# Norm boundaries in two token groups: the last out and down units run once per group, no constant matmuls, five buffers for rounded weights instead of three

## The reference

```python
def rms_norm(x, g):
    y = xf * lax.rsqrt(jnp.mean(jnp.square(xf), axis=-1, keepdims=True) + NORM_EPS)
...
        h_l = modulate(rms_norm(x, g_pre_mix), mod_l[0], mod_l[1])
        p_l = split_proj(h_l @ w_in[l])
...
        y_l = merge_branches((gla_l, att_l, lru_l), p_l[11], w_branch[l], w_out[l])
        x = x + mod_l[2] * rms_norm(y_l, g_post_mix)
...
        h_l = modulate(rms_norm(x, g_pre_ffn), mod_l[3], mod_l[4])
        x = x + mod_l[5] * rms_norm(conv_ffn(h_l, ffn_w_up[l], ffn_conv_w[l], ffn_conv_b[l], ffn_w_down[l]), g_post_ffn)
```

## Time and profile before

| | |
|---|---|
| median of 3 runs | 1924.03 us (1923.77 to 1925.73) |
| the profiled execution, its span | 1924.9 us |
| TensorE busy | 1858.9 us, 97% |
| weight loads (overlap TensorE) | 1545.5 us, 80% |
| VectorE busy | 1343.7 us, 70% |
| ScalarE busy | 990.0 us, 51% |
| transfers | 247.17 MB, mean 128 GB/s |
| mean granted TensorE clock | 0.993 |

### The profile page before, as it was taken

One profiled execution on the slowest core, in us unless ns is written; L12 is line 12 of the kernel. 1 busy time (PEld: TensorE's weight loads), 2 busy tenths in 40 slices (PEclk: granted clock), 3 DMA queues, 4 the chain that ended last, 5 costly groups with the idle time before them and its releaser, 6 DMA issues.

```text
span 1924.9 us, 26001 instructions
## 1 busy us (share of the span) xinstructions
PE 1858.9 (97%) x10504; PEld 1545.5 (80%) x10504; DVE 1343.7 (70%) x1934; ACT 990.0 (51%) x1405; POOL 18.9 (1%) x51
## 2 busy tenths in 40 slices
PE   7999999999999999899999998999999999989998
PEld 4778777777778887578888885778778888979997
DVE  5666546635677887878888797756556688678864
ACT  4543345555665323554444236543446887466663
POOL 1000000000000000000000000000000000000000
PEclk9999999999999999999999999999999999999999
DMA  8211212223244555234444563222323554535653
GB/s 340 70 56 56 72 55 66 77 82 97 90 142 132 181 190 186 98 103 150 164 164 152 188 218 108 77 66 66 93 66 99 155 162 150 183 114 186 181 182 120
DMA packets 68374, 247.17 MB, mean 128 GB/s; under 512 B 7696, under 2 KB 8736, under 8 KB 68128
## 3 DMA queue, kind: packets, MB, share of 16 engines
q1 hardware_dynamic: 65600, 235.96, 37.0%
q0 software_dynamic: 2080, 7.47, 1.3%
q10 hardware_dynamic: 576, 2.10, 0.3%
HBM read 244.44 MB, written 1.05 MB: 128 GB/s over the span
## 4 chain that ended last, share of the span: by engine, by line
PE 72%; DVE 18%; ACT 6%; issue 3%; POOL 0%; ACTq 0%; DVEq 0%; POOLq 0%
PE ps L1499 53%; DVE wlo L842 5%; PE ps L1489 4%; PE ps L1529 2%; DVE fa L892 2%; ACT whi L443 2%; PE ps L1774 2%; PE ps L1869 2%; PE ps L1795 1%; DVE state L1225 1%; PE ps L1707 1%; PE ps L1685 1%; DVE xc L892 1%; PE ps L1786 1%; PE ps L1646 1%
## 5 line engine op out<-in xcount | busy, mean ns | idle before, releaser
L842 DVE TENSOR_TENSOR wlo<-wraw,whi 128x1024 fp32r<-128x1024 f32 x352 | 429.5, 1222 | 235.0 <-ACT whi L443 234.6
L443 ACT ACTIVATE whi<-wraw 128x1024 fp32r<-128x1024 f32 x352 | 370.3, 1054 | 221.8 <-PE ps L1499 208.9
L1499 PE MATMUL ps<-hh,whi 128*128 128x512 f32 (+1 forms) x1632 | 369.3, 348 | 7.3 <-DVE fa L892 3.2
L1499 PE MATMUL ps<-hl,whi 128*128 128x512 f32 (+1 forms) x1632 | 366.0, 346 | 0.0
L1499 PE MATMUL ps<-hh,wlo 128*128 128x512 f32 (+1 forms) x1632 | 335.1, 346 | 1.9 <-DVE wlo L842 1.9
L1499 PEld LDWEIGHTS ps<-hh,whi 128*128 128x128 f32 x1632 | 269.6, 190 | 49.1 <-issue 9.1
L1499 PEld LDWEIGHTS ps<-hl,whi 128*128 128x128 f32 x1632 | 271.2, 190 | 37.6 <-issue 1.6
L1499 PEld LDWEIGHTS ps<-hh,wlo 128*128 128x128 f32 x1632 | 262.7, 190 | 41.1 <-issue 4.4
L870 DVE SCALAR_TENSOR_TENSOR ps<-wada,cond 128x1024 f32<-128x1024 f32 x144 | 173.4, 1246 | 0.0
L892 DVE SCALAR_TENSOR_TENSOR fa<-ps,par,fa 128x510 f32<-128x510 f32 (+1 forms) x176 | 100.1, 610 | 17.2 <-ACT fa L522 15.7
L1499 PE MATMUL ps<-bh,whi 128*128 128x512 f32 (+1 forms) x384 | 88.7, 353 | 0.0
(11 more groups left out here) (300 smaller groups left out, 2592.7 us busy)
## 6 DMA issues: line engine op xcount, KB each, us to landing
wraw<-in_weights SPq DMA_DIRECT2D x352, 512.0 KB, 3.6
wada<-in_w_ada_rows SPq DMA_DIRECT2D x80, 512.0 KB, 3.5
ada_first<-in_w_ada SPq DMA_DIRECT2D x14, 512.0 KB, 16.3
wgate<-in_w_gate POOLq DMA_DIRECT2D x16, 256.0 KB, 2.9
x<-in_xt ACTq DMA_DIRECT2D x2, 512.0 KB, 7.7
x<-in_xt SPq DMA_DIRECT2D x2, 512.0 KB, 7.1
ada_first<-in_w_ada ACTq DMA_DIRECT2D x2, 512.0 KB, 12.5
wdec<-in_w_dec POOLq DMA_DIRECT2D x2, 512.0 KB, 4.8
```

Source lines behind the costliest of these rows:

```text
L443: A_(whi[u % HI][:], wraw[RING_W[u] % RAW][:], ACT.Copy).then_inc(s_hi, 1)
L842: V.tensor_tensor(wlo[s][:], wraw[s][:], whi[u % HI][:].bitcast(F32), ALU.subtract).then_inc(s_lo, 1)
L1499: ins = mm(dst[:, r, c:], w[:, kk, r * P:(r + 1) * P], x_[:, UK * h + kk, c:], start=h == 0 and k in (0, 2) and kk == 0, stop=h == m - 1 a ...
```

## The change

The tokens at a boundary are cut in two groups (`group_of`): context and latent tokens in layer 0 (256 columns each), the two halves of the latent tokens in layer 1 (128 columns each). Each group has its own sums, roots and walk. `last_pair` computes group 0 of the last out or down units, its sums, then group 1 of the last 2 (out) or 3 (down) units; the earlier three units of down run both groups one after the other. The two groups use different PSUM bank pairs. `next_pairs` takes both first pairs through all eight tiles for group 0, then for group 1, with group 1's sums between the first tiles. The constant matmuls are gone. `HI` goes from 3 to 5, for which GpSimd's descriptor scratch becomes smaller. The output leaves in eight transfers of half the size. The low-rank product of gqk moves behind both groups.

```diff
-RAW, HI, LEAD = 7, 3, 2
+RAW, HI, LEAD = 7, 5, 2
+SPLIT = {"out": 2, "down": 3}
...
+        def group_of(m, g):
+            size = CTX if m < 2 else SEQ // 2
+            a = TOK - (2 - g) * size
+            return slice(a, a + size), a // CTX
...
# ScalarE
+                last_tiles(0)
...
+                hi(LATE[m])
+                first_root(0)
+                next_root(0)
+                h(0, 0)
+                h(0, 1)
+                h(0, 2)
+                last_tiles(1)
+                hi(u0 + 2)
+                h(0, 3)
+                h(0, 4)
+                first_root(1)
+                hi(u0 + 3)
+                h(0, 5)
+                h(0, 6)
+                next_root(1)
+                h(0, 7)
+                for k in range(KT):
+                    h(1, k)
...
# VectorE
+                last_cross(0)
                 lo(LATE[m])
...
+                next_sum(0)
+                tile(0, 0)
+                for k in range(1, KT):
+                    tile(0, k)
+                    low(0, k - 1)
+                    if k == 4:
+                        last_cross(1)
+                    if k == 3:
+                        lo(u0 + 2)
+                    if k == 5:
+                        lo(u0 + 3)
+                    if k == 6:
+                        next_sum(1)
+                tile(1, 0)
+                low(0, KT - 1)
+                for k in range(1, KT):
+                    tile(1, k)
+                    low(1, k - 1)
+                low(1, KT - 1)
...
# TensorE, last_pair
-                steps = [(v, k) for ks in ((0, 1, 4), (2, 3, 5)) for v in (u - 1, u) for k in ks]
-                for v, k in steps:
-                    part(v, k)
+                early, late = range(PAIR_UNIT[PAIR_AT[l, name, 3]], u - SPLIT[name] + 1), range(u - SPLIT[name] + 1, u + 1)
+                for v in early:
+                    for g in range(2):
+                        for k in range(6):
+                            part(v, k, g)
+                for v in late:
+                    for k in range(6):
+                        part(v, k, 0)
                 pe.wait_ge(s_adat, len(ADA_MIX) if (l, name) == (0, "out") else len(ADA_TILE))
+                pe.wait_ge(s_acc, 2 * m + 2)
                 for bank, j in banks:
-                    early_sum(l, name, bank, j)
-                    last_sum(l, name, bank, j)
-                if len(banks) == 3:
-                    pe.wait_ge(s_par, 16)
-                    for _ in range(5 if c0_of(l) == 0 else 3):
-                        mm(ps[:, 4, :], ones[:], par[:].rearrange("p l n -> p (l n)")[:, 0:512], start=True, stop=True)
+                    gathered_sum(l, name, bank, j)
+                    last_sum(l, name, bank, j, 0)
+                for v in late:
+                    for k in range(6):
+                        part(v, k, 1)
...
# TensorE, next_pairs
+                one(1, 0, (0,), 0)
+                one(1, 1, (0,), 0)
+                one(1, 0, (1, 2), 0)
+                last_sum(l, name, 6, 0, 1)
+                one(1, 1, (1, 2), 0)
+                for k in range(2):
+                    one(0, k, (0, 1, 2), 0)
+                last_sum(l, name, 7, 1, 1)
+                last_sum(l, name, 5, 2, 1)
+                both(2, (0,), 0)
+                for k in range(2, KT):
+                    if k + 1 < KT:
+                        both(k + 1, (0,), 0)
+                    both(k, (1, 2), 0)
+                both(0, (0,), 1)
+                for k in range(KT):
+                    if k + 1 < KT:
+                        both(k + 1, (0,), 1)
+                    both(k, (1, 2), 1)
+                if n % 2 == 0:
+                    low_rank(n // 2)
```

More of the change, by code:

```diff
@@ L577, in boundary @@
                 squares, scaled_squares, _ = sums_of[name][2]
[L578 to L585, removed]
-                    A_(scaled_squares[:, 0, c0:], branches[:, 0], ACT.Square).then_inc(s_tsq, 1)
-                    hi(LATE[m])
@@ L588, in boundary @@
[L588 to L598 removed]
+                branches = (mixed if name == "out" else y2)[:, 6:8]
@@ new lines, in tile, with low @@
+                def tile(g, k):
+                    c, _ = group_of(m, g)
+                    branch_tile(m, k, src, name, c)
+                    residual_tile(m, g, k, src, c)
+                    scaled_tile(n, g, k, dst, c, root2[name])
+                def low(g, k):
+                    low_tile(n, g, k, dst, group_of(m, g)[0])
+                if m == 2 * DEPTH - 1:
+                    for g in range(2):
+                        c, _ = group_of(m, g)
+                        dve.wait_ge(s_r1, 2 * m + g + 1)
+                        for k in range(0, KT, 2):
+                            two = src[:, k:k + 2, c]
+                            V.tensor_tensor(two, two, root1[name][:, None, c].broadcast_to([P, 2, c.stop - c.start]), ALU.mult)\
+                                .then_inc(s_ym, 2)
+                            dve.wait_ge(s_ym, x_count(m, g, k + 1))
+                            V.tensor_tensor(x[:, k:k + 2, c], x[:, k:k + 2, c], two, ALU.add).then_inc(s_x, 2)
+                    return
@@ L1474, in part @@
                 if k == 0:
-                    if h == 0 and q >= 2:
+                    if h == 0 and group == 1:
+                        pe.wait_ge(taken[(q + 1) % 2], (q + 1) // 2)
+                    elif h == 0 and q >= 2:
                         pe.wait_ge(taken[j], q // 2)
@@ new lines, in last_sum @@
+            def last_sum(l, name, bank, j, g):
+                m = 2 * l + (name == "down")
+                c, _ = group_of(m, g)
+                ready_, n, done = ((s_sq, 2 + 2 * m + g + 1, s_stat), (s_sqp, 5 * m + 4 + g, s_cs),
+                                   (s_xy, 5 * m + 4 + g, s_bs))[j]
+                pe.wait_ge(ready_, n)
+                if g and m < 2 * DEPTH - 1:
+                    pe.wait_ge(s_S, 2 * m + 1)
+                elif g:
+                    pe.wait_ge(s_r1, 2 * m + 1)
+                for t in range(2):
+                    ins = mm(ps[:, bank, c], ones[:], sums_of[name][2][j][:, t, c], start=False, stop=t == 1,
+                             skip_group_check=True)
+                ins.then_inc(done, 1)
@@ new lines, in last_pair, with next_pairs, one, both @@
+                for v in late:
+                    for k in range(6):
+                        part(v, k, 1)
+                if m == 2 * DEPTH - 1:
+                    last_sum(l, name, 6, 0, 1)
+            def next_pairs(u, n):
+                l, name = (n - 1) // 2, "down" if n % 2 == 0 else "out"
+                def one(p, k, which, g):
+                    tile_part(u + 2 * (k // UK) + p, k % UK, n, which, g)
+                def both(k, which, g):
+                    for p in range(2):
+                        one(p, k, which, g)
+                one(1, 0, (0,), 0)
+                one(1, 1, (0,), 0)
+                one(1, 0, (1, 2), 0)
+                last_sum(l, name, 6, 0, 1)
+                one(1, 1, (1, 2), 0)
[15 more added lines that the diff above has]
+                    low_rank(n // 2)
```

310 lines of the change are left out of this document (158 added, 152 removed).

## The result

The changed kernel took 1955.76 us (median of four executions, 1952.45 to 1972.59) against 1924.88 (1923.77 to 1926.41): ratio 1.0175, 95% interval 1.015 to 1.02. That is 31 us slower where 12 were forecast, and above both ranges, 1928 to 1943 and the wider 1917 to 1944. The profiled execution, with a span of 1970.6 us, is the slowest of the four, so its losses are read at their largest; a second profile stands with the experiments.

A forecast was written before the change was run, and what follows sets the result against it. TensorE was taken as the bound, busy 1858.9 of 1924.9 us. Terms -1.5 - 3.0 + 5.5 + 12.9 - 2.0 = +11.9 gave a span of 1936.8, so 1936 us; range 1928 to 1943, 8 in 10 within 1917 to 1944.

The forecast's parts named there:

- B0: Boundary in layer 0, out to up: the groups were to gain, -1.5 us.
- B1: Boundary from layer 0 down to layer 1 gqk: the groups were to gain, -3.0 us.
- B2: Boundary in layer 1, out to up, now 128 columns: the groups were to lose, +5.5 us.
- B3: The end, behind down of layer 1, now 128 columns: the groups were to lose, +12.9 us.
- walk of VectorE 31 us: Layer 0: VectorE's walk over sixteen half tiles was to take 31.0 us against 26.0 before.
- At B2 TensorE without gaps: Expected profile in layer 1, out to up: TensorE sets the pace, VectorE waits; stretch ends at 1739.6 against 1734.07.
- The price of a 128-column matmul: Layer 1's last two boundaries: 0.115 us per matmul, between 0.107 (weight load alone) and 0.120 (with fixed part).
- 81 ns for a sustained matmul of 128 columns: Skill page's figure, an estimate by which the sum would be about 1922 us instead of 1936; no row showed it.
- Five buffers: Rounded weights: ScalarE stops waiting for TensorE before rounding the next unit; -2.0 us (0 to -5).
- Constants: Multiplied constants taken out at three boundaries: their time lies in TensorE's wait for the walk, so 0.
- a slower mode of the short matmul itself: Rival: short matmuls cost 0.22 us as in float32, 58 us more, 1994; chance 13%.

The follow-up runs named there:

- five_buffers_alone: The kernel before with five rounded-weight buffers and the smaller queue scratch, constants kept, no groups: 1923.30 us, ratio 0.999.

## Why the prediction failed, step by step

The direction and the price were right; the time was 19 us above the forecast. Two terms, B0 and B1, had the wrong sign and make 11.4 us of that: B0 came 6.7 us above its term and B1 4.7. B2 makes 2.3 us at full clock and, in the median execution, some 5 more through the half clock (1955.76 against 1950.85 with the pause filled). B3 gives 0.7 back. So two steps failed: "walk of VectorE 31 us", and "At B2 TensorE without gaps" together with the full clock that was assumed there.

- **The price of a 128-column matmul**, 0.115: measured 0.112, and the same at 64 and 192 columns, so the reason given (the weight load) holds. The prediction said that the trace does not show 128 columns; its transposes do, with 0.110. The Trainium skill's 107 ns for a load (TensorE: Matmul & The Clock Gate, section LDWEIGHTS (loading the stationary operand)) agrees; its 81 ns for a sustained matmul of 128 columns (section Back-to-back issue gap), by which 1922 would have come out, does not: here the measurement decides.
- **B3**, +12.9: measured +12.2.
- **B0**, -1.5: +5.2. Sums and the walk's start came as forecast. The walk was 3.8 longer, of which 1.98 + 0.32 + 0.82 are waits for ScalarE. Its rounding of a unit now stands behind group 1's tiles; the order on ScalarE was in the diff and I did not price it. The half clock behind the 3.94 us pause cost 2.9, where 1.4 stood in the sum. With rounding moved and the pause filled, B0 took 55.8 us instead of 58.5, the walk 32.1 instead of 34.8, and the 2.9 were gone.
- **B1**, -3.0: +1.7. The walk's start came as forecast here too, and the walk was 4.4 longer, with the same waits of VectorE for ScalarE in it (2.31 + 0.32 + 0.82). The longer walk is nearly the whole difference of 4.7. Only B0's waits were mended, so the same cause is read from the profile at B1 and not tested.
- **B2**, +5.5: +7.8 at full clock; in the profiled execution 17.8 more through the half clock. The step left out that the two groups hold both bank pairs, so that up waits for ScalarE to empty group 1, and it kept the full clock behind that. I had read the clock of before at B0, and not at B2.
- **Five buffers**, -2.0: -1.9 by the ratio, -3.1 between the medians. Constants, 0: right.
- **The range** had no case in which the clock is lost to the new structure, and it allowed B0 and B1 only 2 us each. Its only way above 1944 was a slower mode of the short matmul itself; 0.22 was nearly the price measured at B2 in such an execution (0.213), but it came from the clock. That this rival named a like number is luck.

Open: at what point of the stream the clock falls in a given execution, and whether B1 would lose nothing with its waits mended. A pause does not always take the clock: in `five_buffers_alone` it is 1.00 in every window from 1700 to 1745, with a pause of 1.53 us ahead of B2's sums.

## What to carry to other kernels

Cutting a matmul to where it streams shorter than its weight load buys nothing: 64, 128 and 192 columns cost the same. When a change reorders one engine, price what the others wait for on it: VectorE's walk came out 3.8 and 4.4 us longer than forecast, most of it waits for ScalarE. Before cutting a product in groups, count the PSUM banks that the groups hold and ask who must empty them before the next product can start. Where narrow matmuls follow a pause, read the granted clock as well as the busy share: TensorE can be busy without a gap and do half the work.

## What the runs showed of the hardware

- A stream of 128-column fp32r matmuls keeps the granted clock (1.00 from 1700 to 1745 with the pause filled), but it did not regain it in 41 us (52 with more of them), though TensorE is busy without a gap. It came back under 512-column fp32r matmuls, 256-column and 192-column ones, and under forty float32 instructions of 128 columns; eight of these did it in one profile and not in the other. With runs of 64-column matmuls between those of 192 columns it fell twice without any pause.
- At half clock a 128-column or 192-column matmul takes 0.213 us, against 0.112 at full clock.
- The same program lost the clock at one point or another of the stretch, and took 1952 to 1973 us. A part of the spread has nothing to do with B2: the first profile has three dips in layer 1 (granted 0.91 over the 20 us from 1360, 1480 and 1620) that the second lacks, and from down3 of layer 0 to out3 of layer 1 they are 562.9 and 558.1 us apart. The profile of before has the first two of these dips.
- A lower mean granted clock need not cost time: without constants and groups it is lower by 0.003. At B1 it is 0.50 from 1180 to 1185, where before had 1.00, and the next wait for VectorE ends at 1191.25 against 1191.15.
